# Context taps of the first tile between the second half's adds, the second tile's convolution behind them: a feed-forward loop on one Trainium2 core

## The chip, the cores and the metric

The kernel runs on one core of one Trainium2 chip. The metric is the device time of one execution in microseconds (us). The kernel before took 3751.31 us, the median of three runs (3750.95 to 3753.1). A further execution was recorded by the profiler; it took 3756.85 us, of which the trace covers a span of 3754.8 us from the first instruction to the last.

## The reference

The reference computes one inference step of a two-layer backbone for 128 context tokens and 1024 latent tokens with 1024 features, in float32. Each layer has a mixer (layer 0: mLSTM heads and retention heads; layer 1: gated linear attention) and a gated feed-forward network with a small depthwise convolution. Only the feed-forward matters here:

```python
def conv_ffn(xn, w_in, conv_w, conv_b, w_out, rows):
    a, v = _split(xn @ w_in, (D_FF, D_FF))          # D_FF = 2816
    if rows is None:                                # context: width-3 convolution over tokens
        a = dwconv_seq(a, conv_w[1])
    else:                                           # latents: 3x3 convolution over a 16 x 64 grid
        a = dwconv_grid(a, conv_w, rows)
    h = jax.nn.gelu(a + conv_b) * v
    return h @ w_out
```

For every feature the convolution has nine taps on the 1024 latent tokens and three taps on the 128 context tokens, twelve in all.

## The kernel before

Tokens lie along the free dimension (T = 1152: 128 context, then 1024 latent), in three groups of 384; features lie on the 128 partitions. Every matrix product is done as three TensorE (PE) passes over operands split in a high and a low part (`wh`, `wl` for weights, `xh`, `xl` or `hh`, `hl` for activations). A weight block of 128 x 1024 is loaded by a DMA into `raw` and split by GpSimd (POOL) into `wh` (L706) and `wl` (L708). There are two buffers, so the split of a block starts when PE has finished the block two before it. A block is 72 matmuls of 384 columns on PE (L725 for all of them).

The feed-forward handles the 22 tiles of 128 hidden features in 11 pairs. For one pair PE runs, in this order: the projection a of tile 0; the first half of the down projection of the *previous* pair; the projection a of tile 1; the second half of that down projection; then the projections v of tile 0 and tile 1. Called here a0, D0, a1, D1, v0, v1. In layer 0, PE also does eight small modulation matmuls (`ada`) behind each projection. The first pair has no D0 and D1 and stands ahead of the loop, so the loop makes ten turns in each layer; what is left of the last pair's down projection (`down_last`) follows behind the loop.

The projections use three PSUM banks (`pj`), which ScalarE (ACT) empties: a into the padded images `pad` (latents) and `padc` (context), v into `vv`. D0 and D1 use a ring of four other banks (`mb`, bank3 to bank6). Each half is 12 groups of 6 matmuls, one bank a group. PE must not start a group before the bank is free (`mb_free`), and VectorE (DVE) frees it by adding the bank to `y` (L2141). So PE can be four groups ahead of DVE, and no more.

DVE executes in the order in which it is written. Its work in one turn of the loop is: 24 adds (12 in `down_half(0)`, 12 in `down_half(1)`); 24 taps of the convolution (`conv_tap`), 12 for each tile, where tap 0 and tap 9 are a plain multiplication (L2112) and the others multiply and add into `cc` (L2114); and for each tile two operations in `value` (L2120, L2122). Taps 0 to 8 work on 128 x 1024 elements, taps 9 to 11 on 128 x 128. Each tap waits for the one before it. Before the change, three taps of tile 0 stand between the adds of D0 and nine behind them; three taps of tile 1 stand between the adds of D1 and nine behind them.

Behind tap 11 of a tile ACT applies gelu to `cc` (L1614, it waits for `conv_done`), then DVE multiplies by `vv`, ACT takes the high part `hh` (L1618) and DVE the low part `hl`. ACT's order in a turn is: `pad` of tile 0, `pad` of tile 1, gelu of tile 0, the three `vv` copies of tile 0 (L1257), gelu of tile 1, `hh` of tile 0, the three `vv` copies of tile 1, `hh` of tile 1. The last copies free the projection banks that the next turn's a0 needs.

Of the kernel before, what the change touches and what calls it, by code (L numbers as in the profile page):

```python
# [374 lines left out]
def build(nc, a):  # L375
# [10 lines left out]
    with ctx:  # L386
# [1352 lines left out]
        def _(dve):  # L1739
# [4 lines left out]
            def link(ins, done=dve_order):  # L1744

                ins.then_inc(done, 1)
                dve.wait_ge(done, n.next(done))

            def give(ins, free):

                ins.then_inc(free, 1)
                n.next(free)
# [5 lines left out]
            def slot():  # L1758
                blocks["n"] += 1
                return (blocks["n"] - 1) % 2  # L1760
# [8 lines left out]
            def full(i):  # L1769
                dve.wait_ge(mb_full[i], n.next(mb_full[i]))  # L1770
# [5 lines left out]
            def tg(c):  # L1776
                return slice(c * TG, (c + 1) * TG)
# [84 lines left out]
            def conditioning(column):  # L1862

                dve.wait_ge(ada_used, n.next(ada_used, 4))
                give(v.tensor_tensor(mod[:, bass.ds(column, 4), :], mb[4][:, 0:8].rearrange("p (c g) -> p c g", g=2),
                                     b3(ada_b[:, bass.ds(column, 4)], 2), ALU.add), mb_free[4])
# [230 lines left out]
            def conv_tap(t, tap):  # L2097

                grid = tap < 9
                i, j = (tap // 3, tap % 3) if grid else (1, tap - 9)  # L2100
                first = tap in (0, 9)
                if grid:
                    src = pad[t][:, i:i + ROWS, j:j + GRID_W]
                    dst = cc[t][:, CTX:T].rearrange("p (r w) -> p r w", w=GRID_W)
                else:
                    src, dst = padc[t][:, j:j + CTX], cc[t][:, 0:CTX]
                w = cw[:, t, 3 * i + j:3 * i + j + 1]
                done = conv_done if tap == 11 else dve_order
                if tap == 0:
                    dve.wait_ge(a_padded, n.next(a_padded))  # L2110
                if first:
                    link(v.tensor_scalar(dst, src, w, None, ALU.mult), done)  # L2112
                else:
                    link(v.scalar_tensor_tensor(dst, src, w, dst, ALU.mult, ALU.add), done)  # L2114

            def value(t):

                dve.wait_ge(gelu_done, n.next(gelu_done))
                dve.wait_ge(v_ready, n.next(v_ready))
                give(v.tensor_tensor(cc[t][:, :], cc[t][:, :], vv[t][:, :], ALU.mult), prod_ready)  # L2120
                dve.wait_ge(hh_ready, n.next(hh_ready))
                link(v.tensor_tensor(hl[:, t, :], cc[t][:, :], hh[:, t, :].bitcast(f32), ALU.subtract), hl_ready)  # L2122

            def act_takes(s):

                n.next(w_used[s])
                for c in range(2):
                    n.next(pj_full[c])

            def down_half(half):  # L2130

                s = slot()
                for m in range(4):
                    for c in range(3):
                        j = 3 * m + c
                        if j == 11:
                            dve.wait_ge(w_used[s], n.next(w_used[s]))
                        else:
                            full(j % 4)
                        dst = y[:, 4 * half + m, tg(c)]  # L2140
                        give(v.tensor_tensor(dst, dst, mb[j % 4][:, 0:TG], ALU.add), mb_free[j % 4])  # L2141
                        if j % 4 == 3:
                            conv_tap(half, j // 4)

            def down_last():
                slots = (slot(), slot())
# [13 lines left out]
            def set_taps(p):  # L2160
                link(v.tensor_copy(cw[:, :, :], conv[:, bass.ds(p * 2, 2), :]))

            def pair(turn, with_down, column, saved=0):
                set_taps(turn)
                for t in range(2):
                    act_takes(slot())
                    if with_down:
                        down_half(t)
                    for tap in range(3 if with_down else 0, 12):
                        conv_tap(t, tap)  # L2170
                if not with_down:
                    dve.wait_ge(x_saved, saved)
                    link(v.memset(y[:, :, :], 0.0))  # L2173
                for t in range(2):
                    act_takes(slot())
                    value(t)
                if column is not None:
                    conditioning(column)

            def ffn(layer):  # L2180
                for t in range(2):
                    link(v.memset(pad[t][:, :, :], 0.0))
                    link(v.memset(padc[t][:, :], 0.0), pads_clear if t else dve_order)
                dve.wait_ge(conv_loaded, n.next(conv_loaded, 16))
                column = 52 if layer == 0 else None
                pair(0, False, column, saved=48 if layer == 0 else 3 * 48)
                with n.loop(dve, f"dve.ffn{layer}", FP - 1) as turn:
                    pair(turn + 1, True, None if column is None else turn * 4 + 56)
                return down_last()
# [206 lines left out]
```

## Time and profile before

| what | us |
|---|---|
| median of three runs | 3751.31 |
| profiled execution, its own time | 3756.85 |
| its span | 3754.8 |
| PE busy | 3391.4 (90%) |
| DVE busy | 1936.1 (52%) |
| POOL busy | 954.3 (25%) |
| ACT busy | 802.2 (21%) |

The loop of layer 0's feed-forward lies in the trace at about 1122 to 1933 us, that of layer 1 at about 2897 to 3667 us. Matmuls overlap in the trace: one of 384 columns shows 0.34 us, but one starts each 0.17 us, so what PE loses is read from the distance of two starts.
### The profile page before, as it was taken

Reading aid. Unit: us, or ns where it says so; the run is one execution under the profiler, and the core shown is the slowest. Engines: PE = TensorE matmul, PEld = TensorE weight load, DVE = VectorE, ACT = ScalarE, POOL = GpSimd, SP = SyncE. Lnnn points to the kernel's source line nnn. Section 1 sums busy time; section 2 is a strip of 40 time slices with the busy share of each in tenths; the row PEclk is TensorE's granted clock in tenths of the full one; section 3 lists DMA queues with packets and bytes.
Section 4 is the critical chain, followed back from the end, with each engine's and each line's share of the span. In section 5 each row is a group of like instructions: output and inputs, shape, how many; then the busy total and the mean of one; then the engine's idle time right before and its main releaser. Section 6 shows DMA issues by size and latency. Waiting matters only on the chain. (4 is left out here: it accounts for less than half of the span.)

```text
span 3754.8 us, 49335 instructions
## 1 busy us (share of the span) xinstructions
PE 3391.4 (90%) x19579; PEld 3300.5 (88%) x19579; DVE 1936.1 (52%) x2395; ACT 802.2 (21%) x1557; POOL 954.3 (25%) x435
## 2 busy tenths in 40 slices
PE   8799989987899999999997897897888999999996
PEld 8788889987899999999997887786788999999995
DVE  1333332222376666655665242445147777677775
ACT  1333331112131111111113332333122111111110
POOL 1111111111223333233321211111212333334330
PEclk8899999988999999999998898998999999999998
DMA  4111111122321111111222001101230111111112
GB/s 163 41 49 57 57 54 54 66 71 79 113 73 63 56 67 56 67 60 68 73 73 86 31 26 36 43 25 36 86 123 30 40 39 45 39 39 39 39 39 101
DMA packets 86089, 225.58 MB, mean 60 GB/s; under 512 B 8000, under 2 KB 45120, under 8 KB 85872
## 3 DMA queue, kind: packets, MB, share of 16 engines
q1 hardware_dynamic: 44064, 163.16, 12.4%
q10 hardware_dynamic: 41936, 61.17, 4.7%
q8 instruction: 64, 1.05, 0.1%
q14 instruction: 25, 0.20, 0.0%
HBM read 193.89 MB, written 30.41 MB: 60 GB/s over the span
## 5 line engine op out<-in xcount | busy, mean ns | idle before, releaser
L725 PE MATMUL bank<-xh,wh 128*128 128x384 f32 x3888 | 1354.2, 348 | 94.1 <-DVE xl L2093 35.6
L725 PE MATMUL bank<-xl,wh 128*128 128x384 f32 x3888 | 1330.0, 342 | 0.0
L725 PE MATMUL bank<-xh,wl 128*128 128x384 f32 x3888 | 1328.3, 342 | 0.0
L706 POOL TENSOR_TENSOR wh<-raw,ones 128x1024 fp32r<-128x1024 f32 x206 | 408.0, 1981 | 2700.4 <-PE bank L725 1753.4
L725 PEld LDWEIGHTS bank<-xh,wh 128*128 128x128 f32 x3888 | 755.5, 194 | 123.3 <-issue 81.3
L725 PEld LDWEIGHTS bank<-xl,wh 128*128 128x128 f32 x3888 | 755.0, 194 | 0.5
L725 PEld LDWEIGHTS bank<-xh,wl 128*128 128x128 f32 x3888 | 752.9, 194 | 0.0
L2114 DVE SCALAR_TENSOR_TENSOR cc<-pad,cw,cc 128x1024 f32<-128x1024 f32 x352 | 597.4, 1697 | 9.7
L708 POOL TENSOR_TENSOR wl<-raw,wh 128x1024 fp32r<-128x1024 f32 x206 | 541.2, 2627 | 16.2
L725 PE MATMUL bank<-hh,wh 128*128 128x384 f32 x1056 | 370.9, 351 | 45.0 <-DVE y L2141 18.3
L2141 DVE TENSOR_TENSOR y<-y,bank 128x384 f32<-128x384 f32 x480 | 255.9, 553 | 300.9 <-PE bank L725 288.7
L725 PE MATMUL bank<-hl,wh 128*128 128x384 f32 x1056 | 365.8, 346 | 0.0
L725 PE MATMUL bank<-hh,wl 128*128 128x384 f32 x1056 | 365.7, 346 | 0.0
L725 PEld LDWEIGHTS bank<-hh,wh 128*128 128x128 f32 x1056 | 205.7, 195 | 52.5 <-DVE y L2141 24.8
L725 PEld LDWEIGHTS bank<-hl,wh 128*128 128x128 f32 x1056 | 205.7, 195 | 0.0
L725 PEld LDWEIGHTS bank<-hh,wl 128*128 128x128 f32 x1056 | 205.3, 194 | 0.0
L1257 ACT ACTIVATE vv<-bank 128x384 f32<-128x384 f32 x132 | 64.1, 489 | 548.1 <-PE bank L725 547.7
L725 PEld LDWEIGHTS bank<-cond,ada_w 128*128 128x128 f32 x1280 | 159.3, 199 | 13.7 <-DMA ada_w<-in_ada 13.7
L725 PE MATMUL bank<-cond,ada_w 128*128 128x2 f32 x1280 | 154.3, 251 | 13.3 <-DMA ada_w<-in_ada 13.3
L1782 DVE TENSOR_TENSOR diag<-bank,ident 128x384 f32<-128x384 f32 x24 | 13.4, 558 | 253.6 <-PE bank L725 253.3
L2120 DVE TENSOR_TENSOR cc<-cc,vv 128x1152 f32<-128x1152 f32 x44 | 72.2, 1640 | 135.5 <-ACT tick L1610 134.7
L725 PE MATMUL bank<-y 128*128 128x128 f32 x1152 | 141.0, 286 | 0.0
(233 smaller groups left out, 2771.5 us busy)
## 6 DMA issues: line engine op xcount, KB each, us to landing
raw<-in_w SPq DMA_DIRECT2D x206, 512.0 KB, 3.3
ada_w<-in_ada SPq DMA_DIRECT2D x80, 512.0 KB, 3.4
residual_scratch<-y ACTq DMA_DIRECT2D x9, 1536.0 KB, 5.8
xg<-residual_scratch ACTq DMA_DIRECT2D x9, 1536.0 KB, 7.8
xr<-mixer_scratch ACTq DMA_DIRECT2D x16, 576.0 KB, 3.8
front<-in_ada SPq DMA_DIRECT2D x16, 512.0 KB, 8.3
y<-in_x SPq DMA_DIRECT2D x1, 4608.0 KB, 19.6
mixer_scratch<-hout ACTq DMA_DIRECT2D x24, 192.0 KB, 1.9
```

What stands on the lines that cost most here:

```text
L706: nc.gpsimd.tensor_tensor(wh[s][:, :], raw[s][:, :], ones[:, 0:1].broadcast_to([128, 1024]), ALU.mult).then_inc(w_hi[s], 1)
L708: nc.gpsimd.tensor_tensor(wl[s][:, :], raw[s][:, :], wh[s][:, :].bitcast(f32), ALU.subtract).then_inc(w_ready[s], 1)
L725: return nc.tensor.matmul(out, lhsT, rhs, start=start, stop=stop)
L1257: fn(out, pj[c][0:out.shape[0], 0:TG], COPY, scale=scale).then_inc(pj_free[c], 1)
L1782: link(v.tensor_tensor(diag[:, :, :], g3(mb[GRAM_BANK[norm]][:, 0:TG]), chunk_row(ident[:, :], 3), ALU.mult))
L2114: link(v.scalar_tensor_tensor(dst, src, w, dst, ALU.mult, ALU.add), done)
L2120: give(v.tensor_tensor(cc[t][:, :], cc[t][:, :], vv[t][:, :], ALU.mult), prod_ready)
L2141: give(v.tensor_tensor(dst, dst, mb[j % 4][:, 0:TG], ALU.add), mb_free[j % 4])
```

## The change

The taps are dealt out to other places; no tap, add or wait is removed or added in number. `down_half` now takes a function `between`, which it calls behind every third add rather than issuing a tap behind every fourth.

```diff
-            def down_half(half):
+            def down_half(half, between):
...
-                        if j % 4 == 3:
-                            conv_tap(half, j // 4)
+                        if j % 3 == 2:
+                            between(j // 3)
...
+                def taps(t, lo, hi):
+                    for tap in range(lo, hi):
+                        conv_tap(t, tap)
+
+                def late(n_):
+                    if n_ < 3:
+                        conv_tap(0, 9 + n_)
+                    else:
+                        conv_tap(1, 0)
+                act_takes(slot())
+                if with_down:
+                    down_half(0, lambda n_: conv_tap(0, n_))
+                    taps(0, 4, 9)
                     act_takes(slot())
-                    if with_down:
-                        down_half(t)
-                    for tap in range(3 if with_down else 0, 12):
-                        conv_tap(t, tap)
+                    down_half(1, late)
+                    taps(1, 1, 12)
+                else:
+                    taps(0, 0, 12)
+                    act_takes(slot())
+                    taps(1, 0, 12)
```

The instructions of PE, ACT, POOL and SyncE keep their order; only DVE's changes. In the listings `cc0`, `pad0`, `padc0` belong to tile 0, `cc1`, `pad1` to tile 1, and the adds are the rows `y<-y,bank`.

DVE where D0's adds end and D1's begin, before:

```order
L2114 SCALAR_TENSOR_TENSOR cc0<-pad0,cw,cc0 128x1024
L1747 REGISTER_ALU
L2112 TENSOR_SCALAR cc0<-padc0,cw 128x128
L1747 REGISTER_ALU
L2114 SCALAR_TENSOR_TENSOR cc0<-padc0,cw,cc0 128x128
L1747 REGISTER_ALU
L2114 SCALAR_TENSOR_TENSOR cc0<-padc0,cw,cc0 128x128
L1770 REGISTER_ALU
L2141 TENSOR_TENSOR y<-y,bank3 128x384
```

The same place now:

```order
L2114 SCALAR_TENSOR_TENSOR cc0<-pad0,cw,cc0 128x1024
L1747 REGISTER_ALU
L1770 REGISTER_ALU
L2141 TENSOR_TENSOR y<-y,bank3 128x384
L2141 TENSOR_TENSOR y<-y,bank4 128x384
L2141 TENSOR_TENSOR y<-y,bank5 128x384
L2112 TENSOR_SCALAR cc0<-padc0,cw 128x128
L1747 REGISTER_ALU
L1770 REGISTER_ALU
L2141 TENSOR_TENSOR y<-y,bank6 128x384
```

The three context taps of tile 0 no longer stand ahead of D1's first add; the first of them now follows D1's third add, the others the sixth and the ninth.

DVE where D1's adds end and the rest of tile 1's convolution begins, before:

```order
L2141 TENSOR_TENSOR y<-y,bank4 128x384
L2141 TENSOR_TENSOR y<-y,bank5 128x384
L2137 REGISTER_ALU
L2141 TENSOR_TENSOR y<-y,bank6 128x384
L2114 SCALAR_TENSOR_TENSOR cc1<-pad1,cw,cc1 128x1024
```

The same place now:

```order
L2141 TENSOR_TENSOR y<-y,bank4 128x384
L2141 TENSOR_TENSOR y<-y,bank5 128x384
L2137 REGISTER_ALU
L2141 TENSOR_TENSOR y<-y,bank6 128x384
L2110 REGISTER_ALU
L2112 TENSOR_SCALAR cc1<-pad1,cw 128x1024
L1747 REGISTER_ALU
L2114 SCALAR_TENSOR_TENSOR cc1<-pad1,cw,cc1 128x1024
```

Behind D1's last add there stood seven full taps of tile 1 and its three context taps; now all nine full taps and the three context taps stand there, beginning with tap 0 (L2112). In D0, likewise, taps 0 to 3 of tile 0 now follow the third, sixth, ninth and twelfth add (before: taps 0 to 2 behind the fourth, eighth and twelfth), so six full taps and no context tap are left between D0's last add and D1's first (before: seven full taps and three context taps).

## Rows read from the trace of the kernel before

**Rows 1.** The page's first part: engine, busy us (share), instructions.

```profile
PE 3391.4 (90%) x19579; PEld 3300.5 (88%) x19579; DVE 1936.1 (52%) x2395; ACT 802.2 (21%) x1557; POOL 954.3 (25%) x435
```

**Rows 2.** Waits, layer 1's loop (2896-3644 us): us in total, times, longest.

```profile
PE bank L725 <- DVE y L2141: 18.3, 10, 1.8
```

**Rows 3.** Waits, layer 0's loop (1077-1933 us).

```profile
PEld bank L725 <- DVE y L2141: 3.3, 10, 0.3
```

**Rows 4.** Timeline of PE, 3079.5-3087 us: start, duration, instruction [idle before <-releaser].

```profile
3080.70 0.34 PE L725 MATMUL bank<-hh,wl 128*128 128x384 f32 x1
3082.87 0.59 PE L725 MATMUL bank<-hh,wh 128*128 128x384 f32 x1 [1.83 <-DVE y L2141]
3083.26 0.53 PE L725 MATMUL bank<-hl,wh 128*128 128x384 f32 x1
...
3086.45 0.34 PE L725 MATMUL bank<-hh,wl 128*128 128x384 f32 x1
```

**Rows 5.** Timeline of PE, 3159.5-3162.5 us.

```profile
3159.61 0.34 PE L725 MATMUL bank<-hh,wl 128*128 128x384 f32 x1
3161.77 0.45 PE L725 MATMUL bank<-hh,wh 128*128 128x384 f32 x1 [1.83 <-DVE y L2141]
3162.06 0.34 PE L725 MATMUL bank<-hl,wh 128*128 128x384 f32 x1
```

**Rows 6.** Stretches: from:to, length, busy of five engines, PEclk, DMA share, GB/s.

```profile
1077.00:1933.00 856.00, 854.80 (x5132) 851.51 (x5133) 552.60 (x559) 120.05 (x232) 287.64 (x124) 1.00 0.18 65
3003.96:3082.87 78.91, 77.08 (x432) 76.76 (x432) 58.03 (x54) 11.02 (x23) 29.16 (x12) 0.98 0.12 40
3161.77:3239.16 77.39, 75.55 (x432) 75.23 (x432) 57.94 (x54) 11.02 (x23) 29.15 (x12) 1.00 0.12 41
```

**Rows 7.** Timeline of DVE, 3131-3189 us.

```profile
3143.74 12.55 DVE L2114 SCALAR_TENSOR_TENSOR cc<-pad,cw,cc 128x1024 f32<-128x1024 f32 x7
3156.33 1.80 DVE L2112 TENSOR_SCALAR cc<-padc,cw 128x128 f32<-128x128 f32 x1
3158.17 2.87 DVE L2114 SCALAR_TENSOR_TENSOR cc<-padc,cw,cc 128x128 f32<-128x128 f32 x2
3161.16 1.95 DVE L2141 TENSOR_TENSOR y<-y,bank 128x384 f32<-128x384 f32 x4
...
3170.53 0.56 DVE L2141 TENSOR_TENSOR y<-y,bank 128x384 f32<-128x384 f32 x1 [0.50 <-PE bank L725]
3171.00 12.55 DVE L2114 SCALAR_TENSOR_TENSOR cc<-pad,cw,cc 128x1024 f32<-128x1024 f32 x7
```

**Rows 8.** Timeline of POOL, 3143-3189 us.

```profile
3143.38 1.90 POOL L706 TENSOR_TENSOR wh<-raw,ones 128x1024 fp32r<-128x1024 f32 x1 [8.36 <-PE bank L725]
...
3155.80 2.25 POOL L706 TENSOR_TENSOR wh<-raw,ones 128x1024 fp32r<-128x1024 f32 x1 [7.20 <-PE bank L725]
3158.13 2.38 POOL L708 TENSOR_TENSOR wl<-raw,wh 128x1024 fp32r<-128x1024 f32 x1
3170.64 1.89 POOL L706 TENSOR_TENSOR wh<-raw,ones 128x1024 fp32r<-128x1024 f32 x1 [10.13 <-PE bank L725]
...
3183.06 2.24 POOL L706 TENSOR_TENSOR wh<-raw,ones 128x1024 fp32r<-128x1024 f32 x1 [7.20 <-PE bank L725]
```

**Rows 9.** Instructions that write `cc`: count, duration ns min/median/max.

```profile
L2114 DVE SCALAR_TENSOR_TENSOR cc<-pad,cw,cc x352: 1277/1285/3310, 1064.2 to 3654.2; 128x1024 f32<-128x1024 f32 x176
L2114 DVE SCALAR_TENSOR_TENSOR cc<-padc,cw,cc x88: 350/352/2514, 1078.6 to 3659.9; 128x128 f32<-128x128 f32 x88
L2112 DVE TENSOR_SCALAR cc<-pad,cw x44: 745/747/1865, 1063.4 to 3633.5; 128x1024 f32<-128x1024 f32 x44
```

**Rows 10.** Timeline of DVE, 3177-3182 us, cut inside the run of seven taps.

```profile
3176.98 5.25 DVE L2114 SCALAR_TENSOR_TENSOR cc<-pad,cw,cc 128x1024 f32<-128x1024 f32 x4
```

**Rows 11.** Timeline of ACT, 3155-3205 us.

```profile
3188.35 1.26 ACT L1614 ACTIVATE cc<-cc,cw 128x1152 f32<-128x1152 f32 x1 [4.75 <-DVE cc L2114]
...
3190.81 1.01 ACT L1257 ACTIVATE vv<-bank 128x384 f32<-128x384 f32 x2
```

More of the change, by code:

```diff
@@ L2164, in pair @@
                 set_taps(turn)
-                for t in range(2):
-                    act_takes(slot())
-                    if with_down:
-                        down_half(t)
-                    for tap in range(3 if with_down else 0, 12):
-                        conv_tap(t, tap)
+                def taps(t, lo, hi):
[10 more added lines that the diff above has]
+                    taps(0, 4, 9)
+                    act_takes(slot())
+                    down_half(1, late)
[4 more added lines that the diff above has]
+                    taps(1, 0, 12)
                 if not with_down:
```

## The prediction

> **What bounds the kernel now.** Read the page's first part first: PE is busy 3391.4 of 3754.8 us, 90%, DVE 52% [rows 1]. So the question for any change on DVE is where PE waits for DVE. The view of waits, cut to the two feed-forward loops, answers it: in layer 1 PE waits ten times for an add of L2141, 18.3 us in all, once in each of the ten turns [rows 2]; in layer 0 only the weight loads show such a wait, ten times, 3.3 us [rows 3]. The timeline of PE shows what one wait looks like: the starts at 3159.61 and 3161.77 lie 2.16 us apart, where 0.17 is usual [rows 5]. The first matmul behind it takes 0.29 rather than 0.17 to the next start. So one wait costs 1.99 + 0.12 = 2.1 us.
>
> The other example shows a second price. At 3082.87 the same wait ends, and the matmuls behind it last 0.53 rather than 0.34 us until 3086.45, where the usual pace returns [rows 4]: PE ran at its lower clock level for some 3.5 us. The view by stretches, from one wait's end to the next, puts a size on it: a turn with such a piece lasts 78.91 us at a mean granted clock of 0.98, one without lasts 77.39 us at 1.00 [rows 6]; the difference is 1.52 us. Of the ten waits of layer 1, seven are followed by slow matmuls (the first at 3003.96, the last at 3632.20), three are not (2926.59, 3161.77, 3397.01). Layer 0's loop, which has no such wait, keeps 1.00 for all its 856 us [rows 6].
>
> Now why DVE is late. In the timelines of DVE and POOL [rows 7, 8], POOL's starts mark the ends of PE's blocks: D0 ends at 3143.38, a1 at 3155.80 (12.42 us for a block), D1 at 3170.64, v0 at 3183.06. From 3143.74 DVE runs seven full taps in 12.55 us; then three context taps, 1.80 us and 2.87 us for two, where one of the latter kind takes 0.35 us when undisturbed [rows 7, 9]. They fall right onto POOL's split of 3155.80 to 3160.51 [rows 8]. So D1's first add starts at 3161.16. Its bank was full one group, 1.04 us, after 3155.80, at 3156.84; PE fills the other three and stands still from about 3159.95, until that add is through.
>
> **What the change does, part by part.**
>
> *Between D0 and D1.* Behind D0's last add now stand six full taps instead of seven, and no context tap. By the same rows: 3143.74 + 12.55 - 1.31 (one undisturbed tap, a quarter of 5.25 [rows 10]) = 3154.98. The bank is full at 3156.84; DVE waits for it with 1.9 us to spare, and PE would stand still only if the first add were not through by about 3159.95, 4.4 us more than the add's 0.55 us after 3154.98. So the waits of layer 1 go: 10 x 2.1 = 21.0 us. In layer 0 the same seven and three taps stand in the same place, with 3.3 us to gain [rows 3]. With the waits the slow pieces go: 7 x 1.52 = 10.6 us.
>
> *In D0*, a full tap now follows each third add instead of each fourth. PE delivers three banks in 3 x 1.04 = 3.1 us. DVE needs for them 3 x 0.49 us back to back (four adds took 1.95 us [rows 7]) plus 1.28 us [rows 9], about 2.8 us: it keeps up. The first tap comes 1.05 us earlier than before and may now fall on POOL's split at the block's start; it then takes up to 1.87 us instead of 0.75 [rows 9]. That makes the next adds about 1 us late, where the ring of four banks allows about 3. Bounds: 0 if the tap misses the split; if the second tap too were caught at its worst (3.31 us, 2.0 more), 3.1 us late, where a wait of a few tenths could begin. I take 0, since the split of 4.3 to 5.2 us is over when the second tap is due, 6.5 us into D0.
>
> *In D1*, context taps follow the adds 3, 6 and 9. Undisturbed they are 0.29 and 0.35 us, at the worst 1.80 and 2.51 [rows 7, 9]; only the first can meet the split. It replaces a tap of 0.75 and one of 1.28 us which stood there. No price.
>
> *Behind D1*, nine full taps instead of seven stand before tile 1's gelu. Here the change adds work to a stretch, and here it could lose. Count from D1's end. Before: seven taps from +0.36 take 12.55 us, the context taps follow, and gelu of tile 1 starts at 3188.35, +17.7 [rows 7, 8, 11]. Now: +0.36 + 0.75 (tap 0) + 12.55 + 1.31 = +15.0 if only the first split is met. But v0 ends at +12.4 and brings the next one; the last two full taps meet it rather than the context taps. Two taps beside a split took 12.55 - 5 x 1.31 = 6.0 us, 3.4 more than alone [rows 7, 10]. Then three undisturbed context taps, 1.05 us: +19.4, nearly 2 us later than before. Who waits? ACT executes in order gelu, `hh` of tile 0, two `vv` copies, which ended at 3190.81 + 1.01, 3.5 us behind gelu's start [rows 11]. The first copy frees the bank that the next a0 needs at v1's end, +24.8. 19.4 + 3.0 for the first copy = +22.4: hidden, with 2.4 us to spare. Bounds: with no split met, +12.7; with all eight multiply-add taps at 3.31, tap 0 at 1.87 and the context taps at their longest (1.80, twice 2.51), +36, and PE would wait 14 us each turn. I take +19.4, from the nearest rows, the same taps beside the same splits.
>
> The Trainium skill has a rule here (SBUF — State Buffer, section "SBUF: two separate sides"): VectorE and GpSimd share one port pair as an exclusive lock, held for a whole instruction, and the loser blocks. By that rule a split, being two instructions, can block two taps at the most, and the +36 cannot occur. The trace agrees: of seven taps beside a split, two took 6.0 us together and the rest 1.31 each [rows 7, 10]. By the worst row alone the sum could lose hundreds of us; by the rule it stays as below.
>
> *Gelu of tile 0* moves from before D1 to behind D1's ninth add, about 10.5 us into it. ACT has nothing else to do until v0's first bank, 4 us behind D1's end. Hidden, with 5 us to spare; beyond that v0's copies would be late.
>
> *The sum.* 21.0 + 3.3 + 10.6 = 34.9 us. Against the profiled execution's own 3756.85 us (span 3754.8, about 2 us around it) that gives 3722. The median of the runs is 5.5 us below the profiled execution; whatever makes that up stands in no row, so I subtract the same sum from it: 3751.3 - 34.9 = 3716.4 us.
>
> **The rivals.**
>
> *The slow pieces stay.* They might come from something other than the waits. For it: three waits in ten have none. Against it: each one begins with the first matmul behind a wait, and 856 us of layer 0 have none. Then only 24.3 us go: 3727.
>
> *The wait moves into D0.* If DVE falls behind by more than the ring there, PE waits at D0's end rather than at D1's start. At half of the old price in layer 1: 3716.4 + 16 = 3732. Against it: DVE's 2.8 us for each 3.1.
>
> *It does not do what it says:* another step holds D1's first add, and the wait stays: 3751. Against it: DVE has no idle time between the taps and that add.
>
> *Slower: the tail behind D1 holds the next a0.* Place: first `vv` copy of tile 1, behind gelu and `hh`. It begins if gelu of tile 1 starts later than +21.8, and eats the whole gain (35 us over 20 turns, 1.75 each) beyond about +23.5. For it: the tail grows by two full taps and meets two splits. If two further splits' worth of blocking came on top (6.8 us, +26.2), each turn would wait 4.4 us: 88 us lost against 34.9 gained, 3804. Against it: 4.1 us lie between +19.4 and +23.5, and there is no third split in that stretch.
>
> **How the numbers follow.** Forecast 3716 (both waits and slow pieces go): 0.78. Slow pieces stay, 3727: 0.09. Wait in D0, 3732: 0.04. No change, 3751: 0.05. Slower, 3804: 0.04. A change of under 0.2%, 7.5 us, cannot be told from none here. Faster by more than that: 0.78 + 0.09 + 0.04 = 0.91; same 0.05; slower 0.04. The range: the forecast may be off by three or so slow pieces elsewhere (1.5 us each) and by some us of what lies behind the loops, so 3708 below; above, it takes in the rival of the slow pieces and ends at 3730.
>
> **What would show it.** In the changed kernel's waits, PE for `y` L2141 should be gone from both loops, or under 3 us in all. The timeline of PE should have no 2 us hole four groups into D1, and no matmuls of 0.53 us in layer 1's loop, whose stretch should show 1.00 and turns of about 75.3 us. On DVE, D1's first add should follow an idle piece of about 2 us that PE ends. Context taps of tile 0 should take 0.35 us in most turns. Gelu of tile 1 should start about 19 us behind D1's end, and PE should not wait for `vv` in the loop. The prediction is wrong if PE waits there or in D0, or if the slow pieces appear without a wait before them.

## The result, and the profile after

The changed kernel took 3720.09 us, the median of four runs (3717.97 to 3724.24), beside 3751.13 us for the kernel before: a ratio of 0.9915 with a 95% interval of 0.9901 to 0.993, a gain of 31.0 us by the medians, 26 to 37 by the interval. Timed a second time it took 3719.42 us beside 3755.26 us, 0.9911 (0.9897 to 0.9924). The forecast was 3716.4 us, a gain of 34.9.

Of the page of the kernel after, the first part (engine, busy us, share, instructions) answers to [rows 1]:

```profile
PE 3379.7 (91%) x19579; PEld 3294.1 (88%) x19579; DVE 1881.3 (51%) x2395; ACT 800.7 (22%) x1557; POOL 942.3 (25%) x435
```

The instructions are the same in number; DVE's work takes 55 us less, because the context taps hardly meet POOL's splits any more: the median of the first of them (L2112 on `padc`) falls from 1.80 to 0.29 us, and none of the others takes more than 0.36 us, where the longest took 2.51 [rows 9]. The full taps meet the splits somewhat more than before: tap 0's median rises from 0.75 [rows 9] to 1.44 us. Whether that is worth anything is for PE's waits to say. In the kernel after, PE's waits in layer 1's feed-forward (2860-3625 us; answers to [rows 2]) and the weight loads' in layer 0's (1077-1933 us; answers to [rows 3]) are these:

```profile
PE bank L725 <- ACT vv L1257: 7.8, 1, 7.8
```

```profile
PEld bank L725 <- ACT vv L1257: 1.1, 1, 1.1
```

No wait for `y` is left in either loop. What is left stands in each layer's first pair, ahead of the loops, and stood there before.

The stretches show what that was worth (from:to, length, busy of five engines, mean granted clock, DMA share, GB/s). The first two run from PE's last wait in the first pair to the end of the last turn's v1, in layer 0 and layer 1; the third of the kernel after is one turn of layer 1, from one first add of D0 to the next. First the kernel before, then the kernel after:

```profile
1108.08:1933.32 825.24, 825.15 (x4945) 821.94 (x4946) 525.30 (x541) 112.71 (x221) 277.87 (x120) 1.00 0.18 65
2880.54:3667.08 786.54, 768.20 (x4319) 765.01 (x4320) 578.96 (x531) 110.50 (x221) 286.31 (x118) 0.98 0.12 39
```

```profile
1108.05:1933.32 825.27, 825.27 (x4945) 825.27 (x4946) 490.60 (x541) 111.65 (x221) 272.60 (x120) 1.00 0.18 65
2881.34:3636.06 754.72, 754.72 (x4320) 754.72 (x4320) 554.81 (x531) 109.50 (x221) 282.86 (x118) 1.00 0.12 40
3123.01:3198.29 75.28, 75.28 (x434) 75.28 (x433) 55.58 (x53) 10.92 (x22) 28.81 (x13) 1.00 0.13 42
```

Layer 1 gained 31.8 us: PE is busy in the whole stretch, the clock is at its higher level throughout, and a turn takes 75.28 us instead of 77.4 or 78.9 [rows 6]. Layer 0 gained nothing in this execution.

The timelines of DVE, POOL and ACT in the kernel after, in one turn of layer 1, answer to [rows 7, 8, 11]:

```profile
3125.59 1.33 DVE L2112 TENSOR_SCALAR cc<-pad,cw 128x1024 f32<-128x1024 f32 x1
...
3135.10 11.23 DVE L2114 SCALAR_TENSOR_TENSOR cc<-pad,cw,cc 128x1024 f32<-128x1024 f32 x6
3148.17 0.56 DVE L2141 TENSOR_TENSOR y<-y,bank 128x384 f32<-128x384 f32 x1 [1.84 <-PE bank L725]
...
3150.75 0.86 DVE L2112 TENSOR_SCALAR cc<-padc,cw 128x128 f32<-128x128 f32 x1
...
3153.92 0.35 DVE L2114 SCALAR_TENSOR_TENSOR cc<-padc,cw,cc 128x128 f32<-128x128 f32 x1
...
3160.26 2.08 DVE L2112 TENSOR_SCALAR cc<-pad,cw 128x1024 f32<-128x1024 f32 x1
3162.37 16.26 DVE L2114 SCALAR_TENSOR_TENSOR cc<-pad,cw,cc 128x1024 f32<-128x1024 f32 x8
```

```profile
3147.15 1.89 POOL L706 TENSOR_TENSOR wh<-raw,ones 128x1024 fp32r<-128x1024 f32 x1 [7.20 <-PE bank L725]
...
3159.90 1.90 POOL L706 TENSOR_TENSOR wh<-raw,ones 128x1024 fp32r<-128x1024 f32 x1 [8.37 <-PE bank L725]
```

```profile
3157.52 1.26 ACT L1614 ACTIVATE cc<-cc,cw 128x1152 f32<-128x1152 f32 x1 [9.83 <-DVE cc L2114]
...
3179.76 1.26 ACT L1614 ACTIVATE cc<-cc,cw 128x1152 f32<-128x1152 f32 x1 [6.91 <-DVE cc L2114]
...
3182.23 0.86 ACT L1257 ACTIVATE vv<-bank 128x384 f32<-128x384 f32 x2
...
3184.75 0.49 ACT L1257 ACTIVATE vv<-bank 128x384 f32<-128x384 f32 x1 [1.67 <-PE bank L725]
```

The reader is to see who waits for whom at D1's start. Before, PE stood still for DVE; now DVE has been idle for 1.84 us when the first bank is full, at 3148.17. In the tail, tap 0 (2.08 us) and the first of the eight multiply-adds (3.30 us) meet the first split, and the last two (2.97 and 3.31 us) meet the second; the five between them take 1.28 us each. So the eight take 16.26 us. Gelu of tile 1 starts at 3179.76, 19.86 us behind D1's end (3159.90), and the first two `vv` copies are through when the third bank of v1 comes: the work that the change put there is hidden.

Why layer 0 shows no gain here is to be read in PE's timeline at the start of its loop:

```profile
1105.23 1.84 PE L725 MATMUL bank<-cond,ada_w 128*128 128x2 f32 x16
1108.05 0.69 PE L725 MATMUL bank<-xh,wh 128*128 128x384 f32 x1 [0.98 <-ACT vv L1257]
1108.54 0.52 PE L725 MATMUL bank<-xl,wh 128*128 128x384 f32 x1
```

Behind a wait of 1 us in the first pair, which the change does not touch, 18 matmuls start at 0.32 us distance rather than 0.17, until 1113.98, and the granted clock of that piece is 0.50, the lower level: about 2.8 us lost. The kernel before has the same wait (ended at 1108.08) and no slow matmuls behind it.

### The profile page after: what moved, and what is told of

The parts are those of the page before. It is cut to its first block and busy times, and to the rows that moved or that the text cites. A ratio compares the mean times of both kernels' runs of the same rounds, so it can differ in the third digit from the quotient of the medians.

```text
span 3722.4 us, 49375 instructions
## 1 busy us (share of the span) xinstructions
PE 3379.7 (91%) x19579; PEld 3294.1 (88%) x19579; DVE 1881.3 (51%) x2395; ACT 800.7 (22%) x1557; POOL 942.3 (25%) x435
## 5 line engine op out<-in xcount | busy, mean ns | idle before, releaser
L706 POOL TENSOR_TENSOR wh<-raw,ones 128x1024 fp32r<-128x1024 f32 x206 | 397.7, 1930 | 2681.3 <-PE bank L725 1729.4
L2114 DVE SCALAR_TENSOR_TENSOR cc<-pad,cw,cc 128x1024 f32<-128x1024 f32 x352 | 608.6, 1729 | 10.4
L725 PEld LDWEIGHTS bank<-y 128*128 128x128 f32 x1152 | 141.8, 205 | 0.0
```

The lines of the kernel that those rows point to most:

```text
L706: nc.gpsimd.tensor_tensor(wh[s][:, :], raw[s][:, :], ones[:, 0:1].broadcast_to([128, 1024]), ALU.mult).then_inc(w_hi[s], 1)
L725: return nc.tensor.matmul(out, lhsT, rhs, start=start, stop=stop)
```

## The experiments

**The changed kernel again.** No edit.

> The changed kernel once more, unaltered. Layer 0's loop ended in the first profile at the same 1933.3 us as in the kernel before, though its waits of 0.3 us a turn were gone; 18 matmuls ran slowly behind a 1 us wait at 1108 us, in the first pair. Theory (that piece follows a wait by chance, in some executions): with it absent layer 0's feed-forward ends 2.8 to 3.3 us earlier; with it present the first profile repeats. Rival (layer 0 gains nothing from the change): its loop takes as long as before though no slow matmuls are in it. Layer 1's loop is without waits and slow matmuls in either case.

It took 3714.41 us, a single run. The same two stretches, and between them the stretch of the second layer's mixer, from the profile of this execution; below it the mixer's stretch of the first profile:

```profile
1931.30:2863.51 932.21, 773.34 (x4208) 722.88 (x4208) 409.63 (x651) 282.31 (x493) 172.49 (x78) 0.90 0.16 56
1108.83:1931.30 822.47, 822.47 (x4944) 822.47 (x4945) 490.35 (x541) 111.67 (x221) 272.47 (x120) 1.00 0.18 65
2871.60:3626.20 754.60, 754.60 (x4320) 754.60 (x4320) 554.80 (x531) 109.50 (x221) 282.90 (x118) 1.00 0.12 40
```

```profile
1933.32:2873.24 939.92, 779.29 (x4208) 727.96 (x4208) 413.56 (x651) 282.44 (x493) 169.30 (x78) 0.90 0.16 55
```

Layer 0's loop is 2.8 us shorter than before (822.47 against 825.24), layer 1's 31.9 us (754.60 against 786.54): 34.7 us together. The 2.8 us of layer 0 are there when no slow piece falls on its start. The stretch between the loops, which the change does not touch, differs by 7.7 us between two executions of one kernel (PE is busy in it 773.34 us in one and 779.29 in the other, with the same 4208 matmuls; the cause stays open), so a difference of a few us between two medians says little, and the stretches say more.

**Only the context taps moved.** All full taps of tile 0 stay where they were before the change; D1 holds nothing but the three context taps of tile 0. Tile 1's first three full taps leave D1 with this edit and stand behind it; they came after D1's first add already, so they cannot be what made it late. `down_half` takes as a third argument how many adds lie between two calls of `between`; without it, three.

```diff
-                    down_half(0, lambda n_: conv_tap(0, n_))
-                    taps(0, 4, 9)
+                    down_half(0, lambda n_: conv_tap(0, n_), 4)
+                    taps(0, 3, 9)
...
-                    down_half(1, late)
-                    taps(1, 1, 12)
+                    down_half(1, lambda n_: conv_tap(0, 9 + n_), 4)
+                    taps(1, 0, 12)
```

> Only the three context taps of tile 0 move, behind the fourth, eighth and twelfth add of D1; D0 is as before the change (full taps behind every fourth add), and all twelve taps of tile 1 stand behind D1. Theory (the late first add of D1 is what PE waits for): the seven full taps end 0.5 us before D1's first bank is full, so PE never waits in the loops, no slow matmuls in layer 1's loop, about 3720 us (3716 to 3726). Rival (the gain needs the closer spacing of taps in D0 and the six-tap stretch): the wait stays in part, at least 1 us a turn in layer 1, 3730 to 3745 us.

Measured: 3724.13 us beside 3755.2, ratio 0.9916 (0.9892 to 0.994). DVE's timeline, at the place of [rows 7]:

```profile
3133.77 12.55 DVE L2114 SCALAR_TENSOR_TENSOR cc<-pad,cw,cc 128x1024 f32<-128x1024 f32 x7
3146.85 0.56 DVE L2141 TENSOR_TENSOR y<-y,bank 128x384 f32<-128x384 f32 x1 [0.52 <-PE bank L725]
```

Seven taps in the very 12.55 us of the kernel before, and DVE is 0.52 us early, as expected. The two loop stretches last 822.48 and 754.57 us, the same as with the whole change. The rival, by which a wait of 1 us a turn stays in layer 1, is out.

**Only a full tap moved.** D0 as in the change, the context taps back ahead of D1, D1 as before.

```diff
-                    taps(0, 4, 9)
+                    taps(0, 4, 12)
...
-                    down_half(1, late)
-                    taps(1, 1, 12)
+                    down_half(1, lambda n_: conv_tap(1, n_), 4)
+                    taps(1, 3, 12)
```

> Only a full tap moves: D0 holds taps 0 to 3 behind every third add, the context taps stay ahead of D1, D1 holds taps 0 to 2 of tile 1 as before the change. Theory (the cost is the meeting of the context taps with POOL's split that begins when a1 ends): six full taps end 0.8 us before the split, the context taps need 1.05 us undisturbed and are through before D1's first bank is full; no wait, about 3720 us (3716 to 3728). Rival (context taps ahead of D1 always meet the split and cost 4.7 us): DVE is free about 3.5 us after a1's end, the wait of PE falls only by about 1.3 us a turn, 3730 to 3745 us.

Measured: 3714.37 us beside 3755.2, ratio 0.9887 (0.9859 to 0.9914). DVE's timeline:

```profile
3128.11 11.23 DVE L2114 SCALAR_TENSOR_TENSOR cc<-pad,cw,cc 128x1024 f32<-128x1024 f32 x6
3139.38 0.29 DVE L2112 TENSOR_SCALAR cc<-padc,cw 128x128 f32<-128x128 f32 x1
3139.70 0.74 DVE L2114 SCALAR_TENSOR_TENSOR cc<-padc,cw,cc 128x128 f32<-128x128 f32 x2
3141.18 0.56 DVE L2141 TENSOR_TENSOR y<-y,bank 128x384 f32<-128x384 f32 x1 [0.74 <-PE bank L725]
```

POOL's split at the same place:

```profile
3140.17 2.02 POOL L706 TENSOR_TENSOR wh<-raw,ones 128x1024 fp32r<-128x1024 f32 x1 [7.20 <-PE bank L725]
```

One tap less ahead of them, and the three context taps take 1.06 us instead of 4.7: the last of them is running when POOL's split begins at 3140.17, and it ends undelayed at 3140.44. The rival, by which they always meet it, is out. The loops last 822.48 and 754.61 us. So each half of the change removes the whole wait; they do not add up. The median lies 1.6 us below the range that was expected, and 10 us below that of the kernel with only the context taps moved; the intervals of the two overlap. Their profiled executions, 5.6 us apart in span, show where such a difference stands. This is the stretch between the loops, up to the end of PE's last wait ahead of layer 1's loop, first with only the context taps moved, then with only the full tap:

```profile
1932.57:2880.16 947.59, 780.79 (x4210) 729.36 (x4209) 416.43 (x653) 283.85 (x496) 176.48 (x80) 0.89 0.16 55
```

```profile
1934.35:2874.46 940.11, 773.61 (x4209) 722.78 (x4209) 416.49 (x653) 283.73 (x496) 176.59 (x80) 0.90 0.16 55
```

That alone makes 7.48 us, in a stretch that neither edit touches, while the loops are equal.

**DVE made late at D1's start.** An unused buffer takes the result of two or three multiply-adds of a full tap's size.

```diff
                     taps(0, 4, 9)
+                    extra(0, 2)        # the other kernel: extra(0, 3)
```

> The changed kernel with two added taps' worth of work (128 x 1024 multiply-adds into an unused buffer, 1.28 us each undisturbed) on DVE between D0's taps and D1's first add, in every turn of both loops; the result of the added work is not used. It gives back part of the 4.4 us that the prediction said DVE may be late there. Theory (ring of four banks, and a tap that meets a split waits for POOL's instruction): the first added tap ends about 0.5 us behind a1's end, the second is held up by the split and ends about 3.5 us behind it; the first add is through just as PE wants its bank: waits of 0 to 0.6 us a turn in layer 1, none in layer 0, few or no slow matmuls, 3714 to 3728 us. Rival (PE waits as soon as DVE is later than the first bank): each turn loses about 2.4 us, 3760 us or more.

> As the kernel with two added taps' worth of work, with three. Theory: the third is held up by the second half of the split and ends about 6.9 us behind a1's end; PE waits about 3.3 us a turn in layer 1 and about 1.4 us in layer 0, 47 us, and slow matmuls (1.5 us a turn or more) come back behind most waits of layer 1: 3770 to 3790 us. Rival (the slow matmuls of the kernel before had another cause than the wait): the waits come, but the loops show no slow matmuls: 3760 to 3765 us.

With two: 3719.2 us. DVE's timeline, and the weight loads' wait in layer 1:

```profile
3127.76 11.23 DVE L2114 SCALAR_TENSOR_TENSOR cc<-pad,cw,cc 128x1024 f32<-128x1024 f32 x6
3139.03 4.12 DVE L2127 SCALAR_TENSOR_TENSOR under_norm<-pad,cw,vv 128x1024 f32<-128x1024 f32 x2
3143.27 1.49 DVE L2148 TENSOR_TENSOR y<-y,bank 128x384 f32<-128x384 f32 x3
```

```profile
PEld bank L725 <- DVE y L2148: 2.4, 10, 0.2
```

The first add comes 4.3 us behind the last tap and costs PE 0.2 us a turn: layer 1's stretch lasts 756.75 us, 2.15 more than the changed kernel's 754.60. The spare time at D1's start is thus about 4 us, as worked out from the ring of four banks. No matmul of the loops ran slowly. The rival, by which each turn loses 2.4 us as soon as DVE is later than the first bank, is out. With three: 3790.18 us, 0.2 us above the expected range. PE's waits in layer 1 (2880-3640 us, nine of the ten turns) and in layer 0 (1115-1933 us), and the two loop stretches:

```profile
PE bank L725 <- DVE y L2148: 29.0, 9, 3.2
```

```profile
PE bank L725 <- DVE y L2148: 14.2, 10, 1.4
```

```profile
1113.91:1953.35 839.44, 825.20 (x4945) 822.00 (x4946) 561.88 (x571) 111.53 (x221) 282.19 (x120) 1.00 0.18 64
2896.86:3700.78 803.92, 771.66 (x4320) 768.47 (x4320) 620.28 (x561) 109.39 (x221) 294.61 (x118) 0.98 0.11 38
```

The third piece of work alone turned 0.2 us into 3.2. All ten waits of layer 1 have slow matmuls behind them; of layer 0's ten waits of 1.42 us none has, and the clock stays at 1.00. Layer 1 lost 803.92 - 754.60 = 49.3 us. A wait of 3.2 us costs about 3.5 (one of 1.83 cost 2.1), so 35 us are the ten waits and 14 the slow matmuls, about 1.4 a turn. The waits and, at this length, the slow pieces can be put back at will; the rival of another cause is out.

**The tail made longer.** The same added work behind D1, ahead of tile 1's other taps: one or three.

```diff
                     down_half(1, late)
+                    extra(1, 1)        # the other kernel: extra(1, 3)
                     taps(1, 1, 12)
```

> The changed kernel with one added tap's worth of work on DVE behind D1's last add and tap 0 of tile 1, ahead of tile 1's other taps, in every turn of both loops; its result is not used. It spends part of the 2.2 us that the tail has left in layer 1. Theory: gelu of tile 1 starts about 21.2 us behind D1's end in layer 1, the first vv copy is through 0.9 us before v1 ends, PE does not wait: 3714 to 3726 us. Rival (the tail already decides when the next turn's a0 starts): each turn loses 1.3 us, 3740 us or more.

> As the kernel with one added tap's worth of work in the tail, with three. Theory: gelu of tile 1 starts about 23.8 us behind D1's end in layer 1, the first vv copy is through about 1.7 us behind v1's end, PE waits there for it in each turn of layer 1, 17 us, some with slow matmuls behind them; layer 0, where the second split comes later, does not wait: 3732 to 3755 us. Rival (the copies are hidden further by a0's second and third bank): no wait of PE for vv in the loops, 3714 to 3726 us.

With one: 3713.05 us, 1 us below the expected range, and PE waits for nothing in layer 1's loop. Gelu of tile 1 starts 21.2 us behind D1's end, as expected. ACT's timeline has the copies through just in time, the second 0.35 us before the third bank is full:

```profile
3169.90 1.26 ACT L1614 ACTIVATE cc<-cc,cw 128x1152 f32<-128x1152 f32 x1 [8.24 <-DVE cc L2114]
...
3172.36 0.85 ACT L1257 ACTIVATE vv<-bank 128x384 f32<-128x384 f32 x2
3173.56 0.49 ACT L1257 ACTIVATE vv<-bank 128x384 f32<-128x384 f32 x1 [0.34 <-PE bank L725]
```

With three: 3759.7 us, about as slow as the kernel before on the same chip (3756.21, one run each). ACT's and PE's timelines, and layer 1's stretch:

```profile
3119.39 1.26 ACT L1614 ACTIVATE cc<-cc,cw 128x1152 f32<-128x1152 f32 x1 [10.88 <-DVE cc L2114]
...
3121.85 1.23 ACT L1257 ACTIVATE vv<-bank 128x384 f32<-128x384 f32 x3
```

```profile
3120.04 0.34 PE L725 MATMUL bank<-xh,wl 128*128 128x384 f32 x1
3122.38 0.57 PE L725 MATMUL bank<-xh,wh 128*128 128x384 f32 x1 [2.00 <-ACT vv L1257]
3122.75 0.52 PE L725 MATMUL bank<-xl,wh 128*128 128x384 f32 x1
```

```profile
2886.15:3669.26 783.11, 765.10 (x4319) 762.20 (x4320) 595.12 (x560) 106.47 (x218) 283.44 (x118) 0.99 0.12 39
```

Gelu of tile 1 starts 23.8 us behind D1's end, as expected. The wait for `vv` is 2.00 us (expected 1.7) in nine turns, five of them with slow matmuls; the tenth turn loses its share behind the loop. Layer 1's stretch is 28.5 us longer than the changed kernel's, layer 0's (822.46 us) not at all. The total came 5 us above the range that was expected. The stretch between the loops, which the edit does not touch, makes up more than that: up to the end of PE's last wait ahead of layer 1's loop it lasts 950.28 us in this execution, against 940.30 in the 3714.41 us execution of the changed kernel. The slower rival of the prediction is thus real, and it begins where it was put: between one and three added taps. The change itself stays short of it by about 2 us.

**The clearing of y moved.** A step that PE waits for outside the loops: in each layer's first pair a memset of `y` stood between the convolution and `value`, for which ACT's copies wait.

```diff
-                if not with_down:
-                    dve.wait_ge(x_saved, saved)
-                    link(v.memset(y[:, :, :], 0.0))
                 for t in range(2):
                     act_takes(slot())
                     value(t)
+                if not with_down:
+                    dve.wait_ge(x_saved, saved)
+                    link(v.memset(y[:, :, :], 0.0))
```

> The changed kernel, with the clearing of y (one 7.7 us memset in each layer's first pair) moved behind the two value steps of that pair. It tests a wait outside the loop by the same reading: ACT's third to fifth step in the first pair waits for value of tile 0, which stands behind that memset, and PE waits 7.8 us (layer 1) and 1.0 us (layer 0) for ACT, with slow matmuls behind it. Theory: both waits go, 8.7 us, and with them some 2 to 5 us of slow matmuls: 3705 to 3711 us. Rival (the next thing in the chain, D0's first add behind the memset, takes the wait's place): 3718 us or more.

> The changed kernel with the clearing of y behind the two value steps of the first pair, timed again on the same chip as the changed kernel. Theory: the stretches of its profile gain 8.6 us in layer 1 and 0.4 us in layer 0, so the median lies about 9 us (6 to 12) below the changed kernel's. Rival (what the first pair gains is given back behind it): within 3 us of the changed kernel.

> The changed kernel, unaltered, timed again beside the kernel with the late clearing. Theory: both loops together gain 34.7 us, as their profiles show stretch by stretch; the median lies 31 to 38 us below the kernel before on the same chip. Rival (about 31 us is the change's full worth, as the first measurement gave, and layer 0's loop gains nothing in the mean): 28 to 31 us.

Measured first: 3710.83 us beside 3755.2, ratio 0.9882 (0.9857 to 0.9907). Then, on one chip: 3711.19 us, 0.9883 (0.9868 to 0.9899), against 3719.42 us for the changed kernel, 0.9911 (0.9897 to 0.9924); 8.2 us between them. It beats both kernels. The new order pays a little back, as PE's timeline shows in layer 1's first turn:

```profile
2882.88 0.45 PE L725 MATMUL bank<-hh,wh 128*128 128x384 f32 x1 [1.00 <-DVE y L2141]
```

The memset now ends late enough for D0's first add of that turn to cost PE 1.0 us, in place of a wait of 7.8 us. In layer 0 the wait of 1 us in the first pair is gone as well, but the stretch behind it is 0.7 us longer than the changed kernel's (823.18 against 822.47). The changed kernel's own gain in this timing is 35.8 us by the medians and 33.4 by the ratio, 28.5 to 38.7 by the interval; the rival of 28 to 31 us is not excluded by the times alone, but no stretch of either loop speaks for it.

## Why the prediction was right, point by point

**What PE waits for**, and the price of one wait. Right. The ten waits of layer 1 are gone with the first add's lateness, and layer 1's stretch is 31.8 to 31.9 us shorter, where 21.0 + 10.6 = 31.6 had been worked out.

**That the slow pieces go with the waits.** Right, and shown: put back a wait of 3.2 us and all ten turns run slowly behind it; without waits none does. The rival of slow pieces that stay is out. One reading given against that rival was not exact: only two of the seven slow pieces begin with the first matmul behind the wait, the other five some tenths of a microsecond later (the wait that ends at 3239.16 has slow matmuls from 3239.98).

**Between D0 and D1.** 1.9 us to spare forecast, 1.84 us measured. The limit of 4.4 us of lateness was sized a little large: at 4.3 us PE already loses 0.2.

**D0.** Price 0. The first tap met POOL's split, as it might, and took 1.33 us (bounds 0.75 and 1.87); no wait followed, so the rival of a wait that moves into D0 is out.

**D1.** The first context tap took 0.86 us, the others 0.35. No price.

**Behind D1.** Gelu of tile 1 at +19.4 forecast, +19.86 measured. That it came so close is in part luck, for two terms were off in opposite directions: tap 0 met the first split and took 2.08 us, where 0.75 had been put in and 1.87 was the bound, and the eight multiply-adds took 16.26, where 12.55 + 1.31 + 3.4 = 17.3 had been put in, because tap 0 had taken one of the two delays of the first split. The taps' worst row of 3.31 us never came eight times in a row: the eight took 5.8 us more than 8 x 1.31. The Trainium skill speaks of an exclusive lock held for a whole instruction (SBUF — State Buffer, section "SBUF: two separate sides"). The trace agrees again: of the nine full taps two were held up by each split (2.08 and 3.30 us, then 2.97 and 3.31), the rest by none.

**Gelu of tile 0.** 10.5 us into D1 forecast; it starts at 3157.52, 10.4 us behind 3147.15. Hidden.

**The sum.** 34.9 forecast, 34.7 in the two loop stretches of the second execution, 31.0 between the first medians, whose interval of 26 to 37 us holds the forecast. The term that was off is layer 0's, 3.3: the loop gives back 2.8 us, and in the first profiled execution that was lost again to a slow piece behind a 1 us wait ahead of the loop. How many of the timed runs had such a piece, the runs do not show. The prediction had said that layer 0 shows no slow matmuls for 856 us; that was so in one execution and not a property of the kernel.

## What to carry to other kernels

Where a fast engine waits for a slow one at a fixed place in a loop, ask for the instruction that is late there and then for what it stands behind: here small taps of 0.3 us that cost 4.7 us because they met another engine's work, and either moving them or starting them 1.3 us earlier removed the whole wait. Spend the work that must be moved on a stretch whose spare time has been worked out from rows, and keep count of it: the tail behind D1 had 4 us to spare, two taps took 2 of it, and three more cost 28.5 of the 34.7 us that the loops had gained. A wait of 2.1 us on PE cost 3.6 us where slow matmuls followed, so a short wait is priced with what runs behind it.

## What the runs showed of the hardware that was not expected

- PE does not always run at its lower clock level behind a wait in these loops: it did so behind none of ten waits of 1.42 us (in layer 0), seven of ten of 1.83 us, five of nine of 2.00 us and ten of ten of 3.2 us (in layer 1). Behind the 1 us wait in layer 0's first pair, with 1.84 us of matmuls of two columns ahead of it, it did so in one of ten profiled executions. A slow piece lasted 2.5 to 6 us and cost 1.1 to 2.8.
- DVE's adds with one input in PSUM take 0.55 us beside a split as well as away from it, while taps with their inputs in SBUF grow from 1.28 us to between 2.5 and 3.3, and context taps from 0.29 to 1.80 and from 0.35 to 2.51.
- Two executions of one kernel differ by 7.7 us in a stretch of 932 us that no edit touches.
